# A two-block transformer kernel on one core: the second block's input norm takes its factor from squares scaled by a root, and each norm's sums share one PSUM bank

## The reference

```python
EPS = NORM_EPS = 1e-6
def rms_norm(x, g):
    return x * rsqrt(mean(x * x, axis=-1) + EPS) * g

def first_block(...):
    ...
    return rms_norm(lat, final_g)            # the first block's last norm

def second_block(x, mem, norm_mix_g, w_in, ...):
    h = rmsnorm(x, norm_mix_g[0])            # the mixer's norm, right behind it
    proj = h @ w_in[0]                       # [256, 1024] @ [1024, 3048]
    ...
    x = x + heads @ w_out[0]
    ...
```

## Time and profile before

| what | value |
|---|---|
| median of 3 timed runs | 1637.15 us |
| lowest, highest | 1634.83 us, 1640.71 us |
| span of the profiled execution, first to last instruction | 1636.5 us |
| the profiled execution's own time | not given apart from its span; the span stands 0.65 us under the median and within the three runs |
| TensorE busy, weight loads busy | 94%, 83% |
| VectorE, ScalarE, GpSimd busy | 69%, 49%, 8% |
| mean granted TensorE clock | 0.976 |
| HBM over the span | 140 GB/s |

### The profile page before, as it was taken

How to read it: one execution, slowest core, us unless ns; L and a number is a source line. 1 busy time by engine, 2 the same in 40 slices (tenths; PEclk the granted TensorE clock), 3 DMA queues, 4 the chain that set the end, 5 groups by cost and what they waited for, 6 DMA issues and landing times.

```text
span 1636.5 us, 30942 instructions
## 1 busy us (share of the span) xinstructions
PE 1545.0 (94%) x11438; PEld 1366.0 (83%) x11438; DVE 1131.6 (69%) x1901; ACT 799.3 (49%) x1437; POOL 123.0 (8%) x139
## 2 busy tenths in 40 slices
PE   5899998899899999999899999999999889999998
PEld 2688888888688888878786699999898669999997
DVE  5986866554798888887735478875666765577654
ACT  3545554242554544322445467774445445666532
POOL 2000052512000000010000010001000001000000
PEclk9999999999899999999899999999899999999999
DMA  9345510002254445565431045556454214255552
GB/s 367 115 173 180 182 54 1 3 2 78 91 180 167 163 170 175 172 218 208 171 120 52 1 149 186 182 192 216 150 162 142 88 65 142 89 186 190 183 189 90
DMA packets 62956, 230.78 MB, mean 141 GB/s; under 512 B 6800, under 2 KB 8080, under 8 KB 62352
## 3 DMA queue, kind: packets, MB, share of 16 engines
q1 hardware_dynamic: 61408, 223.37, 39.9%
q0 software_dynamic: 1168, 5.80, 1.1%
q10 hardware_dynamic: 288, 0.33, 0.1%
HBM read 228.43 MB, written 1.05 MB: 140 GB/s over the span
## 4 chain that ended last, share of the span: by engine, by line
PE 85%; DVE 9%; ACT 3%; issue 2%; DMA 1%; POOL 0%; SPq 0%; DVEq 0%; ACTq 0%; POOLq 0%
PE proj L653 23%; PE proj L655 23%; PE proj L654 22%; PE bank L912 1%; DVE w_low L2156 1%; ACT w_high L1638 1%; PE bank L705 1%; DMA a_first<-a_stream 1%; PE bank L929 1%; PE bank L932 1%; DVE mod_products L2265 1%; PE proj L1134 1%; DVE h_low L2189 1%; DVE tmp L2200 1%; PE bank L961 1%
## 5 line engine op out<-in xcount | busy, mean ns | idle before, releaser
L653 PE MATMUL proj<-h_high,w_high 128*128 128x256 f32 (+1 forms) x1776 | 583.5, 329 | 20.8 <-DVE h_low L2189 14.6
L655 PE MATMUL proj<-h_high,w_low 128*128 128x256 f32 (+1 forms) x1776 | 571.8, 322 | 0.0
L654 PE MATMUL proj<-h_low,w_high 128*128 128x256 f32 (+1 forms) x1776 | 570.1, 321 | 0.0
L2156 DVE TENSOR_TENSOR w_low<-w_raw,w_high 128x1024 fp32r<-128x1024 f32 x322 | 393.3, 1224 | 152.6 <-ACT w_high L1638 151.2
L1638 ACT ACTIVATE w_high<-w_raw 128x1024 fp32r<-128x1024 f32 x322 | 338.3, 1055 | 233.1 <-PE proj L655 227.4
L653 PEld LDWEIGHTS proj<-h_high,w_high 128*128 128x128 f32 x1776 | 337.3, 190 | 56.6 <-issue 18.3
L655 PEld LDWEIGHTS proj<-h_high,w_low 128*128 128x128 f32 x1776 | 337.7, 190 | 27.6
L654 PEld LDWEIGHTS proj<-h_low,w_high 128*128 128x128 f32 x1776 | 337.2, 190 | 25.5
L653 PE MATMUL proj<-act_high,w_high 128*128 128x256 f32 (+1 forms) x608 | 190.7, 314 | 0.1
L655 PE MATMUL proj<-act_high,w_low 128*128 128x256 f32 (+1 forms) x608 | 189.7, 312 | 0.0
L654 PE MATMUL proj<-act_low,w_high 128*128 128x256 f32 (+1 forms) x608 | 189.1, 311 | 0.0
(11 more groups left out here) (411 smaller groups left out, 1889.0 us busy)
## 6 DMA issues: line engine op xcount, KB each, us to landing
w_raw<-w_stream SPq DMA_DIRECT2D x322, 512.0 KB, 3.3
a_ring<-a_stream SPq DMA_DIRECT2D x80, 512.0 KB, 4.1
a_first<-a_head SPq DMA_DIRECT2D x4, 1024.0 KB, 17.9
a_first<-a_stream SPq DMA_DIRECT2D x4, 1024.0 KB, 18.5
x<-x_in SPq DMA_DIRECT2D x1, 2048.0 KB, 10.5
late_tab<-late_tables POOLq DMA_DIRECT2D x1, 1408.0 KB, 6.6
cond_rows<-cond_rows SPq DMA_DIRECT2D x1, 1024.0 KB, 5.9
cond_rows<-cond_rows POOLq DMA_DIRECT2D x1, 1024.0 KB, 5.0
```

The costliest lines, as they stand in the source:

```text
L653: mm(out_, wh, xh, start=first, stop=False)
L654: mm(out_, wh, xl, start=False, stop=False)
L655: return mm(out_, wl, xh, start=False, stop=last)
L2156: v.tensor_tensor(wl(n), RAW[:, n % 4, :], wh(n), ALU.subtract).then_inc(w_low, 1)
```

## The change

Three things change.

**The mixer's factor.** At the start of stage `dn1` ScalarE makes eight columns sqrt(g² + eps) from `final_g` (two linked instructions, L1702 and L1703 of the changed kernel) and uses them as the scale of `mix`'s squares. The sums are then those of x²·(g² + eps), and root (with eps² as the bias) and reciprocal give the mixer's factor at once. The two scalings, the root behind them and the product are gone; `final1`'s factor is made by itself, behind the mixer's, and spread into bank 1 by its own.

**The order of the sums.** Chunk by chunk instead of norm by norm: `mix` 0, `final1` 0, `mix` 6, `final1` 6, `mix` 7, `final1` 7.

**One bank for a norm's sums.** Every norm's token groups lie in neighbouring columns of one bank (bank 0, and bank 2 for `final1` when summed with `mix`). Only the first matmul of a norm has `start`, and ScalarE reads all columns in one instruction.

```diff
@@ norm_sum (TensorE)
-            def norm_sum(name, c=0, count=1):
+            def norm_sum(*names):
...
-                    for t in range(width // P):
-                        last = mm(SUMS[t][:, c:c + 1], squares(name, k)[:, t * P:(t + 1) * P], ONES[:, 0:1], start=(k == 0), stop=(k == nch - 1))
-                if count:
-                    last.then_inc(n_ss, count)
+                    for c, name in enumerate(names):
+                        if early and k == 0:
+
+                            pe.wait_ge(n_early, (EARLY - 1) * (SUMMED.index(names[-1]) + 1))
+                        else:
+
+                            pe.wait_ge(n_sq, sq_count(name, k))
+                        for t in range(width // P):
+                            o = BK[2 * c][:, t:t + 1]
+                            last = mm(o, squares(name, k)[:, t * P:(t + 1) * P], ONES[:, 0:1], start=(k == 0 and t == 0), stop=(k == nch - 1 and t == width // P - 1))
+                        if k == nch - 1:
+                            last.then_inc(n_ss, 1)
...
@@ behind stage dn1 (TensorE)
-            norm_sum("mix", 1, 0)
-            norm_sum("final1", 0, 2)
-            pe.wait_ge(n_std, NORM_I["mix"] + 2)
-            for c, x in ((10, CTX), (8, LAT)):
+            norm_sum("mix", "final1")
+            for c, name in enumerate(("mix", "final1")):
+                pe.wait_ge(n_std, NORM_I[name] + 1)
                 for t in range(2):
-                    o = BK[0][:, x.start + t * P:x.start + (t + 1) * P]
-                    last = mm(o, STD[:, c + t:c + t + 1].to_broadcast([P, P]), ID[:], start=True, stop=True)
-            last.then_inc(n_bc, 2)
+                    last = mm(BK[c][:, t * P:(t + 1) * P], STD[:, 8 + 2 * c + t:9 + 2 * c + t].to_broadcast([P, P]), ID[:], start=True, stop=True)
+                last.then_inc(n_bc, 1)
...
@@ norm_root (ScalarE)
-                for t in range(width // P):
-                    last = f(STD[:, t:t + 1], SUMS[t][:, 0:1], ACT.Sqrt, scale=1.0 / features, bias=col("eps"))
-                last.then_inc(n_root, 1)
+                nt = width // P
+                f(STD[:, 0:nt], BK[0][:, 0:nt], ACT.Sqrt, scale=1.0 / features, bias=col("eps")).then_inc(n_root, 1)
...
@@ chunk_squares and residuals (ScalarE)
-                    f(squares("mix", k), norm_src("mix", k), ACT.Square, scale=col("final1", k)).then_inc(n_sq, 1)
+                    f(squares("mix", k), norm_src("mix", k), ACT.Square, scale=SM[:, 72 + k:73 + k]).then_inc(n_sq, 1)
...
+                if then == "final1":
+                    link(f(SM[:, 72:80], C[:, COL_AT["final1"]:COL_AT["final1"] + KC], ACT.Square))
+                    link(f(SM[:, 72:80], SM[:, 72:80], ACT.Sqrt, bias=col("eps")))
...
@@ behind residuals("dn1", 3, "final1") (ScalarE)
-            act.wait_ge(n_ss, NORM_I["mix"] + 2)
-            for t in range(2):
-                last = f(STD[:, t:t + 1], SUMS[t][:, 0:1], ACT.Sqrt, scale=1.0 / D, bias=col("eps"))
-            last.then_inc(n_root, 1)
-            act.wait_ge(n_std, NORM_I["mix"] + 1)
-            f(STD[:, 2:4], STD[:, 16:18], ACT.Sqrt, scale=1.0 / D, bias=col("eps")).then_inc(n_root, 1)
+            for c, name, small in ((0, "mix", "eps_squared"), (2, "final1", "eps")):
+                act.wait_ge(n_ss, NORM_I[name] + 1)
+                f(STD[:, c:c + 2], BK[c][:, 0:2], ACT.Sqrt, scale=1.0 / D, bias=col(small)).then_inc(n_root, 1)
...
@@ two_norms (VectorE)
-                v.tensor_tensor(gain, C[:, COL_AT["final1"]:COL_AT["final1"] + KC], C[:, COL_AT["mix"]:COL_AT["mix"] + KC], ALU.mult)
-                dve.wait_ge(n_root, i + 1)
-                link(v.reciprocal(STD[:, 8:10], STD[:, 0:2]))
-                for t in range(2):
-                    last = v.scalar_tensor_tensor(STD[:, 16 + t:17 + t], SUMS[t][:, 1:2], STD[:, 8 + t:9 + t], STD[:, 8 + t:9 + t], ALU.mult, ALU.mult)
-                last.then_inc(n_std, 1)
-                dve.wait_ge(n_root, i + 2)
-                link(v.reciprocal(STD[:, 18:20], STD[:, 2:4]))
-                v.tensor_tensor(STD[:, 10:12], STD[:, 18:20], STD[:, 8:10], ALU.mult).then_inc(n_std, 1)
-                dve.wait_ge(n_bc, i + 2)
+                link(v.tensor_tensor(gain, C[:, COL_AT["final1"]:COL_AT["final1"] + KC], C[:, COL_AT["mix"]:COL_AT["mix"] + KC], ALU.mult))
+                for c, name in ((0, "mix"), (2, "final1")):
+                    dve.wait_ge(n_root, NORM_I[name] + 1)
+                    v.reciprocal(STD[:, 8 + c:10 + c], STD[:, c:c + 2]).then_inc(n_std, 1)
+                dve.wait_ge(n_bc, NORM_I["mix"] + 1)
```

More of the change, by code:

```diff
@@ L42 @@
         ("a_ln_g", 4), ("a_ln_b", 4), ("b_norm", 1), ("mla_q", 3), ("mla_kv", 2), ("fconv", 2 * 2 * FC * 3),
-        ("final1", 8), ("mix", 8), ("kv2", 1), ("cross", 8), ("mem", 8), ("mlp", 8), ("final2", 8), ("eps", 1), ("one", 1)]
+        ("final1", 8), ("mix", 8), ("kv2", 1), ("cross", 8), ("mem", 8), ("mlp", 8), ("final2", 8), ("eps", 1), ("one", 1), ("eps_squared", 1)]
 COL_AT = {}
@@ L232, in lay_out @@
             vec(a["final_g"]), vec(a["norm_mix_g_2"][0]), vec(a["kv_norm_g_2"][0]), vec(a["norm_cross_g_2"][0]),
-            vec(a["norm_mem_g_2"][0]), vec(a["norm_mlp_g_2"][0]), vec(a["norm_final_g_2"]), np.full((P, 1), EPS, f), np.ones((P, 1), f)]
+            vec(a["norm_mem_g_2"][0]), vec(a["norm_mlp_g_2"][0]), vec(a["norm_final_g_2"]), np.full((P, 1), EPS, f), np.ones((P, 1), f),
+            np.full((P, 1), EPS * EPS, f)]
     gdn, late = tables()
@@ L321, in two_blocks_kernel @@
         STD = place("std", [P, T2])
-        SM = place("small", [P, 72])
+        SM = place("small", [P, 80])
         XP = place("conv_in", [P, 2, 2, SEQ + 2])
@@ L484, in two_blocks_kernel @@
         ROWS = [(BK[0], BK[1]), (PL[0], PL[1])]
-        SUMS = [BK[i] for i in (0, 2, 3, 4)]
         OUT_BANKS = (PL, BK[0:2])
@@ L691, in h_ready @@
                 return lambda k: (n_lo, NORM_S0[name] + k + 1)
-            def norm_sum(name, c=0, count=1):
-                _, nch, width = NORMS[NORM_I[name]]
-                chunks = [0, *range(EARLY, nch)] if name in SUMMED else range(nch)
+            def norm_sum(*names):
+                _, nch, width = NORMS[NORM_I[names[0]]]
+                early = names[0] in SUMMED
+                chunks = [0, *range(EARLY, nch)] if early else range(nch)
                 for k in chunks:
[L698 to L703, removed]
-                    for t in range(width // P):
-                        last = mm(SUMS[t][:, c:c + 1], squares(name, k)[:, t * P:(t + 1) * P], ONES[:, 0:1], start=(k == 0), stop=(k == nch - 1))
-                if count:
-                    last.then_inc(n_ss, count)
+                    for c, name in enumerate(names):
[8 more added lines that the diff above has]
+                            last.then_inc(n_ss, 1)
             def norm_spread(name):
@@ L1266, in index_logits @@
                     po, w = 64 * (h % 2), (1 + c // 8) * P
+                    if c == 0:
+                        pe.wait_ge(n_xn, NORM_X0["final1"] + KC)
                     if c >= 2:
@@ L2702, in _ @@
                     continue
+                if m == 20:
+                    dve.wait_ge(n_bc, NORM_I["final1"] + 1)
                 for k in range(4 * (m - 20), 4 * (m - 20) + 4):
                     x = X[:, k, LAT]
-                    v.scalar_tensor_tensor(x, x, col("final1", k), BK[0][:, LAT], ALU.mult, ALU.mult).then_inc(n_xn, 1)
+                    v.scalar_tensor_tensor(x, x, col("final1", k), BK[1][:, CTX], ALU.mult, ALU.mult).then_inc(n_xn, 1)
             def index_sum(b):
```

1 line of the change is left out of this document (removed).

## The result

The changed kernel has a median of 1646.34 us in five runs (1645.26 to 1648.10). The kernel before has 1639.61 us, its three runs and two more beside those of the changed kernel together (1634.83 to 1640.71). The ratio is 1.0051 with a 95% interval of 1.004 to 1.0062: slower, by 6.7 us, where 1632.8 us was predicted.

What follows compares the result with a forecast made beforehand. The kernel was taken as bound by TensorE, with time won only where it stands still. Terms 3.59 + 0.90 + 0.42 − 0.55 = 4.36 us, from 1637.15, gave 1632.8 us; range 1630.3 to 1636.6.

Steps and rivals of the forecast that it cites:

- the extra column in the table of columns: Column added to the table of columns, said to lie under the first transfers and priced at nothing.
- the slower one: Norm sums accumulating in neighbouring columns of one bank stall TensorE; about 1655 us if each waits; chance 0.05.
- The added pair: Square and Sqrt at the start of `dn1` delay the first weight block: 0.55 us lost, bounds 0.40 and 0.70.
- The mixer's part: Behind `dn1`, reordered sums and one root and reciprocal start the first scaled chunk 3.59 us earlier.
- the 3.08: Gain in us behind `dn1` if the factors' spread falls on the low clock, taking 1.22 us, not 0.71.
- The shared bank: One root per norm saves 0.90 us at `n2_0` and `n1_1`, 0.42 at `n2_1`, `mem` and `final2`: 1.32 us.
- The rival of the clock: Behind `dn1` the shorter pause leaves the clock high, 1.5 us more gained, 1631.3 us; chance 0.15.
- the 6.8 us that the forecast had: Length of the low clock stretch at `n2_1`, put at the shorter pause behind `dn1`; no change in the sum.
- The gain given back in `in2`: Weight transfers do not start earlier, so products in `in2` wait; 0.77 us of gain left, 1636.4 us; chance 0.20.
- The price of a root: At the norms, the second, third and fourth root add 0.15 us each, since they overlap; one costs 0.27 us.
- The estimate of 2.7 us: Saving at three two-root and two four-root norms by the skill page's 0.3 us per ACTIVATE; time near 1631.4 us.

Runs made afterwards that it cites:

- experiment 1: Only the width of `small` changed: kernel before at 80 columns 1652.50 us, at 88 columns 1652.03; changed kernel at 88 columns 1644.09, at 96 columns 1644.46.
- experiment 2: Changed kernel with `small` back at 72 columns and the eight factors in unused columns of `std`, so no tensor moves: 1632.91 us, ratio 0.9965 to the kernel before.
- experiment 3: Changed kernel at the old layout, with the linked Square and Sqrt behind the first three weight blocks of `dn1`: 1630.60 us, ratio 0.9958 to the kernel before.
- experiment 4: Kernel before plus only the change at the `mix` norm, old layout, other norms keeping four banks and own roots: 1635.24 us, ratio 0.9982 to the kernel before.

## Why the prediction was wrong

**The step that failed** is the one that priced the new columns. It said that "the extra column in the table of columns lies under the first transfers: nothing", and had no term at all for the eight columns of `small`, nor for TensorE's pace. That term is +13.0 us (experiment 1), three times the whole sum of 4.36; with the 6.2 us that the edits gain at that layout it gives 6.8 us, the measured loss of 6.7. None of the rivals held it: the slower one, adding up in one bank, is refuted, for 20 sum matmul records behind `dn1` took 2.14 us in the rows above (0.107 each), and the products run at the old pace with one bank and the old layout (experiment 2).

**The other terms.** The ruler gives each place its step: how much longer (+) the time between the weight splits on either side of it is than in the kernel before. At the old layout nothing is added in between, so experiments 2, 3 and 4 show the terms alone. Behind `dn1`, for instance, ScalarE's timeline has of the kernel before

```profile
1150.06 1.06 ACT L1638 ACTIVATE w_high<-w_raw 128x1024 fp32r<-128x1024 f32 x1 [1.76 <-PE proj L655]
...
1168.10 1.05 ACT L1638 ACTIVATE w_high<-w_raw 128x1024 fp32r<-128x1024 f32 x1
```

and of experiment 2 the same two splits

```profile
1149.13 1.06 ACT L1640 ACTIVATE w_high<-w_raw 128x1024 fp32r<-128x1024 f32 x1 [1.76 <-PE proj L654]
...
1163.50 1.05 ACT L1640 ACTIVATE w_high<-w_raw 128x1024 fp32r<-128x1024 f32 x1
```

18.04 us before, 14.37 us there: −3.67, in the table −3.66 from the unrounded times.

| place | predicted us | exp. 2 | exp. 3 | exp. 4 |
|---|---|---|---|---|
| `n2_0` | −0.45 | −0.80 | −0.51 | −0.01 |
| `n1_1` | −0.45 | −0.87 | −0.87 | +0.34 |
| `mem` | −0.14 | −1.34 | −1.48 | −0.01 |
| `n2_1` | −0.14 | −0.22 | −0.21 | −0.06 |
| start of `dn1` | +0.55 | +0.55 | 0.00 | +0.55 |
| behind `dn1` | −3.59 | −3.66 | −3.49 | −3.75 |

- **The added pair** (+0.55) was right, and so were its parts. ScalarE's timeline of the changed kernel has the Square, the Sqrt and the first weight split 0.23 and 0.33 us apart, each with its handover; the forecast had 0.20 and 0.31 and 0.04 for the handovers:

```profile
1102.57 0.20 ACT L1702 ACTIVATE small<-cols_sb 128x8 f32<-128x8 f32 x1
1102.80 0.30 ACT L1703 ACTIVATE small<-small,cols_sb 128x8 f32<-128x8 f32 x1
1103.13 2.95 ACT L1640 ACTIVATE w_high<-w_raw 128x1024 fp32r<-128x1024 f32 x3
```

- **The mixer's part** (−3.59) was right to 0.2 us in these steps, and its sum with the pair in the measured time too (experiment 4), but that is partly luck. The forecast put the spread on the high clock, and in the changed kernel it is. In experiments 2, 3 and 4 the clock fell just before the spread began. Experiment 2, the last squares in the timeline:

```profile
1152.29 0.40 ACT L1656 ACTIVATE tmp<-x 128x256 f32<-128x256 f32 x1
```

  the chain of waits behind them:

```profile
1153.89 1.24 PE bank L1246 x4
...
1155.15 0.49 DVE tmp L2221
...
1156.69 0.55 PE proj L652
```

  and the stretches, with the clock at 1.00, 0.50 and 1.00:

```profile
1151.50:1153.30 1.80, 1.80 (x18) 1.80 (x18) 0.41 (x2) 0.81 (x2) 1.16 (x3) 1.00 0.56 157
1153.60:1160.20 6.60, 5.85 (x26) 5.49 (x26) 5.29 (x16) 3.07 (x8) 0.60 (x1) 0.50 0.34 122
1160.30:1162.30 2.00, 2.00 (x19) 2.00 (x18) 1.32 (x4) 1.37 (x2) 0.00 (x0) 1.00 0.04 12
```

  The first scaled chunk stands 2.47 us behind the last squares (1.96 in the changed kernel), so the pause is 3.15 us shorter, near the 3.08 that the prediction gave for this case and did not take. What makes up for it is that the low stretch ends 3.6, 4.0 and 3.3 us behind the start of the products in experiments 2, 3 and 4, where it ended 4.7 us behind it before. Half of the difference, 0.4 to 0.7 us, comes back. In the changed kernel both are the other way round: the pause is 3.66 us shorter, the low stretch ends 5.4 us behind the start of the products, and the step is only −3.31 us.
- **The shared bank** was sized too low. Predicted were 1.32 us, the steps of experiment 3 add up to 3.1 us at four places. Most of the surplus is `mem`, and there it is the clock: its low stretch lasts 3.4 us in all five profiles with one bank for that norm, in place of 6.8 us in nine of the twelve without. But the other three of those twelve have 3.4 us as well, with steps of −1.18 to −1.37 us and no change in code at this place. So the shorter chain makes the shorter stretch likelier, and is not needed for it. Of the step at `n1_1`, 0.42 us are not accounted for (the low stretch is 10.2 us in both; the +0.34 in experiment 4 goes with one of 13.7 us). At `final2` nothing can be told from zero.
- **The rival of the clock**, a clock that stays high, did not come about behind `dn1`; what came back there is the 0.4 to 0.7 us above. The stretches there, of the changed kernel, answer to the earlier trace rows:

```profile
1162.00:1164.20 2.20, 2.02 (x19) 1.94 (x18) 0.36 (x3) 0.74 (x3) 1.72 (x3) 1.00 0.91 309
1164.40:1166.40 2.00, 1.03 (x5) 0.76 (x5) 1.91 (x6) 1.22 (x3) 0.00 (x0) 0.50 0.37 148
1170.00:1171.00 1.00, 1.00 (x7) 1.00 (x6) 0.42 (x1) 0.99 (x2) 0.00 (x0) 0.50 0.03 8
1171.10:1172.00 0.90, 0.90 (x9) 0.90 (x9) 0.90 (x1) 0.00 (x0) 0.00 (x0) 0.99 0.00 0
```

  The clock fell between 1164.2 and 1164.4 and rose by 1171.1: the 6.8 us that the forecast had, where 10.2 us stood before. All six profiles with the mixer's part have 6.8 us, nine of the eleven without 10.2; the other two have 6.8 with the old chain, so the shorter pause isn't needed for it.
- **The gain given back in `in2`** is refuted: in experiment 2 the lead over the kernel before is 4.60 us at block 210 and 4.81 us at block 315, in experiment 3 7.40 and 7.61.
- **The price of a root.** The rows went on to disagree with what the prediction quoted of the Trainium skill ("ScalarE: Activation LUTs", Rules for kernel authors, about 0.3 us for each ACTIVATE) where roots overlap. After the change one root reads the four columns of `n2_0` in 0.26 us, where four took 0.72:

```profile
419.87 0.26 ACT L1664 ACTIVATE std<-bank,cols_sb 128x4 f32<-128x4 f32 x1 [1.14 <-PE bank L707]
```

  The estimate of 2.7 us by that page of the Trainium skill lies nearer to the 3.1 us of the steps, but almost half of those is `mem` with its clock.

At the old layout the forecast would have held: 1632.91 us measured, 1632.8 predicted (a gain of 5.0 us over the 1637.93 beside it, 4.36 predicted). Part of that is luck: the steps of experiment 2 add up to −6.3 us, and in its profile the stages before block 30 took 1.6 us more than in the kernel before, where neither the code nor the layout differs by more than a root.

## What to carry to other kernels

Read every line of a diff that allocates, above all one that only widens a scratch tensor: everything placed behind it moves, and products at full pace changed here by up to 2% in either direction. Eight columns were worth 13 us, about twice the 5.0, 6.2 and 7.9 us that the edits gained at three layouts. When a kernel is slower where its code is the same, lay the two traces over each other by an instruction that both have in one order, and see whether the difference grows step by step (a wait) or steadily (a pace). Before judging any small edit, put new columns into free space of an old tensor, or pad to 256 bytes (which gave the old pace back here), so that the comparison is of the edit alone. And small instructions whose inputs are known early go behind the first weight blocks of a stage, not ahead of them (0.55 us here).

## What the runs showed of the hardware

- The pace of a stream of fp32 products changed with where the tensors lie in SBUF: 265.1 to 273.1 us for the same 1165 products of 512 columns, 110.6 to 114.3 us for 959 records of 256 columns, the same again after 256 bytes, and the best place for one width (192 bytes) was the worst for the other. For the wide products it is the place of the moving operand relative to the weight buffers (267.4 us when both moved by 32 bytes, 272.1 to 272.4 when one did); for the narrow ones this was not separated from the absolute address. Whether TensorE's weight loads, the splits of VectorE and ScalarE or something else meets its reads is open; no run took the splits away.
- The low stretch of the granted clock at one place was 3.4 us in some traces and 6.8 us in others (`mem`), or 10.2 and 13.7 us (`n1_1`), with the same code there; at `mem` that is worth 1.2 to 1.4 us. Behind `dn1` the clock fell 0.5 to 2.1 us after the last squares in the six profiles with the mixer's part, so that the spread of the factors took 0.7 us in two of them and 1.2 in four. Terms under 1 us can be read from the step at their place, hardly from two totals.
